# The conv branch's output product by seven block products instead of eight, its second-half gates read back half a tile at a time

## What is computed

```python
h = rmsnorm(x, norm_mix)
proj = h @ w_in + b_in                        # val, gate, pool_in, gate_a, gate_b
u = val * sigmoid(gate)
u = silu(layernorm(causal_dwconv31(u)))       # z below
ya = u @ conv_w_out                           # the product that is changed, 1024 x 1024 x 1024
yb = pool_branch(pool_in)                     # trailing means, one map per group
merged = sigmoid(gate_a) * ya + sigmoid(gate_b) * yb
x = x + merged @ mix_w_out                    # "the mix"
x = x + gdfn(rmsnorm(x))                      # up-projection, conv of 3, gelu * gate, down-projection
return rmsnorm(x)
```

## Time and profile before

| what | us |
|---|---|
| median of 3 runs (1289.60 to 1290.78) | 1289.91 |
| the profiled execution | 1289.33 |
| its span, first to last instruction | 1287.3 |
| PE busy | 1270.3 |
| DVE busy | 1022.8 |
| POOL busy | 871.1 |
| ACT busy | 479.5 |

### The profile page before, as it was taken

The page is one execution under the profiler, slowest core; times in us unless marked ns, Lnnn a source line. Parts: engine busy times, 40 slices in busy tenths (PEclk is TensorE's granted clock), DMA queues, the critical chain, the costliest instruction groups (busy, mean ns, idle before and its releaser), DMA issues.

```text
span 1287.3 us, 15571 instructions
## 1 busy us (share of the span) xinstructions
PE 1270.3 (99%) x5766; PEld 1053.8 (82%) x5766; DVE 1022.8 (79%) x1163; ACT 479.5 (37%) x691; POOL 871.1 (68%) x579
## 2 busy tenths in 40 slices
PE   8999999999999999999999999999999999999997
PEld 8888888888888778877888888888888888888887
DVE  5898989999999784589677767677666779887975
ACT  6211221213234580143445343343344445424551
POOL 4536637665787833478739977877887876567861
PEclk9999999999999999999999999999999999999999
DMA  9411121214334372344212322332232259868923
GB/s 352 149 33 49 34 82 49 82 33 164 99 99 149 130 290 69 114 155 164 102 39 90 123 107 92 121 121 88 93 117 107 90 175 361 332 243 290 367 87 131
DMA packets 66408, 179.26 MB, mean 139 GB/s; under 512 B 4896, under 2 KB 13088, under 8 KB 62496
## 3 DMA queue, kind: packets, MB, share of 16 engines
q1 hardware_dynamic: 61888, 167.82, 36.2%
q10 hardware_dynamic: 4448, 10.49, 2.2%
HBM read 137.14 MB, written 41.16 MB: 139 GB/s over the span
## 4 chain that ended last, share of the span: by engine, by line
PE 90%; DVE 4%; ACT 2%; issue 2%; POOL 1%; DMA 1%; SPq 0%; DVEq 0%; POOLq 0%; ACTq 0%
PE ps L2494 30%; PE ps L2495 30%; PE ps L2496 30%; DMA cv<-in_x 1%; DVE h_lo L2092 1%; POOL w_lo L1037 1%; PE ps L2558 1%; ACT cv L1244 0%; PE ps L2548 0%; DVE cv L2083 0%; ACT cv_r L1626 0%; DVE hi_f L2004 0%; POOL w_lo L1170 0%; DVE res L2271 0%; DVE res L2187 0%
## 5 line engine op out<-in xcount | busy, mean ns | idle before, releaser
L2494 PE MATMUL ps<-h_lo,w_hi 128*128 128x512 f32 (+1 forms) x900 | 348.0, 387 | 4.5 <-DVE h_lo L1838 1.9
L2496 PE MATMUL ps<-h_hi,w_hi 128*128 128x512 f32 (+1 forms) x900 | 345.9, 384 | 0.0
L2495 PE MATMUL ps<-h_hi,w_lo 128*128 128x512 f32 (+1 forms) x900 | 345.9, 384 | 0.0
L2494 PEld LDWEIGHTS ps<-h_lo,w_hi 128*128 128x128 f32 x900 | 169.0, 188 | 41.8 <-DVE h_lo L1838 3.1
L2496 PEld LDWEIGHTS ps<-h_hi,w_hi 128*128 128x128 f32 x900 | 169.0, 188 | 33.9
L2495 PEld LDWEIGHTS ps<-h_hi,w_lo 128*128 128x128 f32 x900 | 169.1, 188 | 33.1
L1918 DVE SCALAR_TENSOR_TENSOR ps<-tmp,par,ps 128x512 f32<-128x512 f32 x224 | 158.5, 750 | 0.0
L965 POOL TENSOR_SCALAR w_hi<-raw 128x1024 fp32r<-128x1024 f32 x32 | 36.5, 1141 | 156.1 <-issue 127.5
L2494 PE MATMUL ps<-ga_r,w_hi 128*128 128x512 f32 (+1 forms) x303 | 117.4, 388 | 0.3 <-POOL w_lo L1170 0.3
L2496 PE MATMUL ps<-cv_r,w_hi 128*128 128x512 f32 (+1 forms) x303 | 117.1, 386 | 0.0
L2495 PE MATMUL ps<-cv_r,w_lo 128*128 128x512 f32 (+1 forms) x303 | 117.0, 386 | 0.0
(11 more groups left out here) (308 smaller groups left out, 2721.3 us busy)
## 6 DMA issues: line engine op xcount, KB each, us to landing
raw<-in_wstream SPq DMA_DIRECT2D x54, 512.0 KB, 3.5
tmp<-in_wffn SPq DMA_DIRECT2D x14, 1024.0 KB, 4.7
g_kept<-res SPq DMA_DIRECT2D x21, 512.0 KB, 2.8
res<-in_wffn SPq DMA_DIRECT2D x10, 1024.0 KB, 4.8
ga_r<-g_kept SPq DMA_DIRECT2D x18, 512.0 KB, 7.0
h_lo<-g_kept SPq DMA_DIRECT2D x17, 512.0 KB, 7.5
res<-in_xT SPq DMA_DIRECT2D x7, 1024.0 KB, 5.8
g_kept<-raw SPq DMA_DIRECT2D x12, 512.0 KB, 2.9
```

Source lines behind the costliest of these rows:

```text
L2494: nc.tensor.matmul(out, a_hi, b_lo, start=start, stop=False, skip_group_check=onto)
L2495: nc.tensor.matmul(out, a_lo, b_hi, start=False, stop=False, skip_group_check=onto)
L2496: return nc.tensor.matmul(out, a_hi, b_hi, start=False, stop=stop, skip_group_check=onto)
```

## The change

The conv branch's output product is done by seven products over four pairs of output tiles too. P1 and P2 run for all four pairs; the other five for pairs 0 and 1 and then for 2 and 3. POOL makes its weight sums and lows (28 + 16 operations of 128x512), ACT its 28 highs, DVE its T sums, T lows and posts. Its T2 stays in PSUM (four banks), T1, T3 and T4 lie in `ga` and `cv`. The gates come back as 16 half tiles into four slots in `cv`, each asked for when the merge four places before has multiplied. The merged tiles are merged by halves, and their splits go to `h_hi` and `h_lo` half by half. The lists of calls are rewritten accordingly, those of the mix's start too; the weight block for the mix's pair 1 lies in `raw`.

```diff
+CONV_SEQ = [(p, i) for p in (P1, P2) for i in range(MP)]
+CONV_SEQ += [(p, a + i) for a in (0, 2) for p in (P6, P5, P7, P4, P3) for i in range(2)]
+MERGES = [(what, a + i) for a in (0, 2) for what in ("c11", "c22", "c21", "c12") for i in range(2)]
...
+        def conv_t2(k):
+            return bank((4, 5, 6, 1)[k])
+        def conv_bank(p, i):
+            if p in (P1, P2):
+                return bank((2, 3, 7, 0)[i])
+            return bank(((4, 5), (6, 1))[i % 2][p in (P5, P3)])
...
+            def gates_back(j):
+                what, i = MERGES[j]
+                m, h = 2 * i + int(what[1]) - 1, int(what[2]) - 1
+                if j == 0:
+                    sp.wait_ge(z_lo, KT + KT // 2)
+                    sp.wait_ge(t_sum, CONV_TS + 2 * KT)
+                if j >= 4:
+                    sp.wait_ge(co_a, j - 4 + 1)
...
+                sp.dma_start(a_slot[j % 4], a_dram[:, m, h * HALF:(h + 1) * HALF]).then_inc(pos_loaded[j % 4], 16)
...
+            for j in range(4):
+                gates_back(j)
+            for i in (2, 3):
+                sp.wait_ge(f_sum, conv_summed(i - 2, "S4"))
+                load_conv_quarter(i, 0, f_wlo, conv_op(P6, i - 2) + 1)
+            gates_back(4)
+            gates_back(5)
+            for i in (2, 3):
+                load_conv_quarter(i, 2, f_wlo, conv_op(P7, i - 2) + 1)
+            for i in (2, 3):
+                load_conv_quarter(i, 3, f_wlo, conv_op(P4, i - 2) + 1)
...
-            for s, i in enumerate((1, 3)):
-                sp.wait_ge(f_wlo, mix_op(P2, i) + 1)
+            sp.wait_ge(f_wlo, mix_op(P3, 1) + 1)
+            for s in range(2):
                 load_weights(N_FFN + s)
...
+            conv_low(P1, 0)
+            conv_sum("S1", 0)
+            conv_sum("S3", 0)
+            conv_low(P1, 1)
+            conv_sum("S2", 0)
+            conv_sum("S1", 1)
+            conv_sum("S3", 1)
+            conv_low(P1, 2)
+            conv_low(P1, 3)
+            conv_sum("S2", 1)
+            for i in range(MP):
+                conv_low(P2, i)
...
                 if what == "S1":
-                    pool.wait_ge(mx_c[i], 16)
-                    if i == 3:
-                        pool.wait_ge(f_used, mix_op(P1, 3) + 1)
+                    pool.wait_ge(mx_c[i], 48)
+                    if i == 0:
+                        pool.wait_ge(co_m, len(MERGES))
...
             z_high(0, 0, 1)
             ln_silu(7)
-            z_high(0, 2, 3, 4, 5, 6, 7)
-            z_high(1, 0, 1, 2, 3, 4, 5, 6, 7)
+            z_high(0, 2, 3)
+            conv_high(P1, 0)
+            conv_high(P1, 1)
+            z_high(0, 4, 5, 6, 7)
+            conv_high(P1, 2)
             gate_a1(5)
...
             ln_scaled(7)
+            for k in range(4):
+                conv_t_sum("T1", k)
             z_low(0, 0, 1, 2, 3)
+            for k in range(2):
+                conv_t_sum("T3", k)
             gate_c21(5)
+            for k in range(2, 4):
+                conv_t_sum("T3", k)
+            gate_c12(5)
+            for k in range(4):
+                conv_t_sum("T2", k)
             z_low(0, 4, 5, 6, 7)
-            gate_c12(5)
-            z_low(1, 0, 1, 2, 3, 4, 5, 6, 7)
             gate_pooled(5)
+            z_low(1, 4, 5)
+            for k in range(4):
+                conv_t_sum("T4", k)
+            z_low(1, 6, 7)
+            for k in range(4):
+                conv_t2_low(k)
+            conv_t_low("T1")
...
+            conv_u2_of(2)
+            merged_low(0, 0)
+            merged_low(1, 0)
+            conv_u2_of(3)
+            merge("c11", 2)
+            merge("c11", 3)
+            merged_low(2, 0)
+            merged_low(3, 0)
+            for k in range(4):
+                mix_t_sum_of("T1", k)
+            conv_c22(2)
+            merge("c22", 2)
+            merged_low(4, 0)
+            conv_c22(3)
...
+            conv_c12(3)
+            merge("c12", 3)
+            mix_t_sum_of("T3", 2)
+            for m in (5, 7, 4, 6):
+                merged_low(m, 1)
+            for k in (1, 3, 0, 2):
+                mix_t_sum_of("T2", k)
...
+            for k in (1, 3):
+                mix_t_sum_of("T4", k)
             mix_t_low("T3")
+            for k in (0, 2):
+                mix_t_sum_of("T4", k)
             mix_add("P2 0 11")
             mix_t_low("T2")
...
-            pairs(N_OUT, (((f_post, gate_posted(GP - 2, "c12")),),
-                          ((s1_out, gates_read(GP - 1, 1)), (f_post, gate_posted(GP - 1, "c21")))), co_m, h_hi, h_lo,
-                  lambda h, k: (z_lo, KT * h + k + 1))
+            for i in range(MP):
+                pe.wait_ge(*((f_post, gate_posted(GP - 2, "c21")), (f_post, gate_posted(GP - 2, "c12")),
+                             (s1_out, gates_read(GP - 2, 1)), (s1_out, gates_read(GP - 1, 1)))[i])
+                conv_product(P1, i, ready=(lambda k: (z_lo, k + 1)) if i == 0 else None)
+            for i in range(MP):
+                pe.wait_ge(f_v1, GP + i + 1)
+                conv_product(P2, i, False, ready=(lambda k: (z_lo, 4 + k + 1)) if i == 0 else None)
+            for a in (0, 2):
+                for i in (a, a + 1):
+                    if a:
+                        pe.wait_ge(co_m, merged("c21", i - 2))
+                    elif i == 0:
+                        pe.wait_ge(t_sum, CONV_TS + 2 * KT)
+                        pe.wait_ge(t_lo, CONV_THS + KT // 2)
+                    conv_product(P6, i)
...
```

More of the change, by code:

```diff
@@ L55 @@
 N_OUT = 5 * KT
-N_FFN = N_OUT + KT
+N_FFN = N_OUT
 N_UP = 2 * PLAIN
@@ new lines, in build, with conv_weights, z_part @@
+        a_slot = [cv[:, 6 * SEQ + i * HALF:6 * SEQ + (i + 1) * HALF] for i in range(4)]
+        def conv_weights(p, i):
+            if p == P1:
+                return block_quarter(i, 0) if i < 2 else csum[:, span(i - 2)[0]:span(i - 2)[1]]
+            if p == P2:
+                return block_quarter(i, 1) if i < 2 else second_half(lo_f, i)
+            return conv_s1[i % 2] if p == P5 else block_quarter(i, {P6: 0, P3: 1, P7: 2, P4: 3}[p])
+        def z_part(c, h):
+            return together(tile(cv, c))[:, h * PART:(h + 1) * PART, :]
@@ new lines, in _ @@
+            conv_first(1)
+            conv_high(P2, 1)
+            z_high(1, 6, 7)
+            conv_t2_high(0)
+            conv_t2_high(1)
+            conv_first(2)
+            conv_high(P2, 2)
+            conv_t2_high(2)
+            conv_t2_high(3)
+            conv_first(3)
+            conv_high(P2, 3)
+            conv_high(P6, 0)
+            conv_t_high("T1")
+            conv_high(P6, 1)
+            conv_t_high("T3")
+            conv_high(P5, 0)
+            conv_t_high("T4")
+            for p, i in CONV_SEQ[CONV_SEQ.index((P5, 1)):CONV_SEQ.index((P4, 1)) + 1]:
+                conv_high(p, i)
@@ new lines, in _ @@
+            conv_u2_of(0)
+            conv_t_low("T3")
+            conv_u2_of(1)
+            conv_t_low("T4")
+            merge("c11", 0)
+            merge("c11", 1)
+            for i in range(2):
+                conv_c22(i)
+                merge("c22", i)
+            for i in range(2):
+                conv_c21(i)
+                merge("c21", i)
+            for i in range(2):
+                conv_c12(i)
+                merge("c12", i)
+            conv_u2_of(2)
+            merged_low(0, 0)
@@ new lines, in _ @@
+            merged_low(1, 0)
[10 more added lines that the diff above has]
+            conv_c22(3)
+            merge("c22", 3)
+            conv_c21(2)
+            merge("c21", 2)
+            mix_t_sum_of("T3", 1)
+            merged_low(5, 0)
@@ L2959, in lay_out @@
         pairs.append(block)
-    pairs += [np.concatenate([mix[2 * i], mix[2 * i + 1]], axis=1) for i in range(MP)]
+    pairs += [np.concatenate([w[2 * i], w[2 * i + 1]], axis=1) for w in (out, mix) for i in range(MP)]
+    for half in (slice(0, HALF), slice(HALF, CH)):
+        pairs.append(np.concatenate([mix[2 * i][:, half] for i in range(MP)], axis=1))
     ffn_stream = np.ascontiguousarray(np.concatenate(pairs, axis=0))
```

606 lines of the change are left out of this document (412 added, 194 removed).

## The result

The changed kernel takes 1305.8 us (median of 4 runs, 1305.5 to 1307.2), the kernel before beside it 1289.8; the ratio is 1.0124, 95% interval 1.0111 to 1.0136. So it is 16.0 us slower; the forecast was 11.1 above the median of before. The profiled execution took 1305.5, its span is 1303.7, 16.4 more than the span of before.

A forecast was written before the change was run, and what follows sets the result against it. TensorE was taken to bound the kernel. Saved matmuls (10.88 us) were outweighed by waits at the conv start (12.0), middle (3.7) and mix (10): +11.3 on 1289.33 gave 1300.6, as median 1301; range 1286 to 1306.

The forecast's parts named there:

- Start, steps 1 and 2: Conv stage's start: POOL's first split at 467.3, P1 0 at 469.0; eight POOL operations make P1 2 4.7 to 8.3 late.
- a sign that I had put under "wrong": Signs against the forecast: T sums of 0.7 beside busy POOL, T2's into PSUM at 0.7, POOL's first split before 467.
- signs for "right": Conv start: PE idle 8 to 10 us before P1 1, P1 2, P2 0; DVE's T sums and z lows at 1.7.
- Start, step 3: Conv start: DVE's queue alternates with POOL, z_low(0,7) ends at 490.3, P2 0 waits at its fourth step; P2 3 10.2 late.
- Start, step 4: Conv start: P6 0 waits for T sums and four T2 lows until 501.1, 12.0 late; 8.5 if PSUM-writing T2 is free.
- Middle: Rest of the conv stage: waits at P7 0 1.0, P6 2 0.7, P4 2 0.9, P4 3 1.1; sum 3.7, from 0 to 7.
- Last merge: Between conv stage and mix: c12(3) merged about 5 us behind the stage's end, at 564.
- The chain: DVE behind the last merge: 27 us beside POOL, to 591, a stall of 10; without POOL it would end in time.
- Behind the T2 product: After the mix's first T2 product: same order as before, 1 off for POOL's full ring, 0.3 added for up-projection weights.
- absorbed: Rival: operations of DVE and POOL meet less than the queues suggest, start costs only 4.8; 1283.5 us, chance 0.20.
- The mix in time: Rival: earlier last merge or POOL idling between mix sums leaves 4 to 6 of 10; chance 0.22, shared with T2 free.
- Late loads: Rival: quarters for S1 1 or behind gates 4 and 5 land late, S1 and P6 2 wait 5 to 8 more; chance 0.08.

The follow-up runs named there:

- start_mid: Changed kernel with start_order's order at the conv stage's start, mended, and POOL's splits P3 1 and P6 2 moved ahead of sums mid-stage; 1305.9 us.
- mix_psum: Changed kernel with the DVE operations behind the last merge reading their second operand from PSUM instead of SBUF (values not right); 1292.0 us.
- both_psum: Changed kernel with the edits of t_psum and mix_psum together, no order changed (values not right); 1289.8 us, ratio to the kernel before 1.0003.
- mix_hold: mix_order with POOL also held behind the split of P4 0 until DVE's T2 low in the mix; 1303.3 us.
- mix_order: Changed kernel with POOL's mix sums for pair 0 made between the splits of P1, and P2 0's copy and split before the last merges; 1304.0 us.
- keep_busy: Changed kernel with useless matmuls of 512 columns put into the places where PE waits; 1309.7 us.
- t_psum: Changed kernel with the conv branch's T1, T3 and T2 sums reading one operand from PSUM instead of SBUF (values not right); 1301.6 us.
- start_order: Changed kernel with the same operations in another order on POOL, DVE and ACT at the conv stage's start; 1305.8 us.
- all_orders: Changed kernel with the edits of start_mid and mix_hold together, no operation added or removed; 1302.8 us.

## Why the forecast came out as it did

The direction and the main mechanism were right, and the sum was 4.8 too small. The measured time is just inside the upper bound of 1306. In the profile the span grew by 16.4 where the sum has 11.3, 5.1 more: start -0.6, middle +2.3, last merge +2.9, chain -0.9, PE's start behind the chain +0.1, behind the T2 product +1.2. Terms that were 6.5 too small stand against 1.5 that was too large. Step by step:

- **What is removed**: 48 matmuls, as counted.
- **Start, steps 1 and 2.** Forecast: POOL's first split at 467.3, P1 0 at 469.0, P1 2 late by 4.7 to 8.3. Measured: the split starts earlier, at 466.69, but lasts 3.66, so P1 0 starts at 470.45, and P1 2 at 482.46, 9.7 late. I had let an operation of POOL take 1.7 at most when DVE is full. So a sign that I had put under "wrong" (a first split before 467) did come, and no gain with it. The signs for "right" came in part: PE idles 2.8 before P1 0 and 3.4 before P1 2, not before P1 1 or P2 0, together 6.2 and not 8 to 10.
- **Start, step 3.** Wrong place: z_low(0,7) was to end at 490.3 and to stop P2 0 at its fourth step. It ended at 486.3, and P2 0 did not wait. P1 2 and P1 3 had been late enough. start_mid shows the limit of step 4 by itself: with P1 and P2 on time, P6 0 would still come at 495.3.
- **Start, step 4.** Right to 0.6 us (501.1 forecast, 500.48 measured), partly by luck, since it was POOL's order that set it, not DVE's chain: P6 0 follows P2 3 without a wait, 1.2 after the last T2 low (499.24). In DVE's chain two errors met: it reached the end of z_low(0,7) 4.0 early, and from there to the last T2 low it took 13.0 where I had 10.8. The value I chose for T2's sums in PSUM was right: they took up to 1.8 and 1.66 in the mean, and 0.70 once one input was in PSUM too. The Trainium skill (SBUF — State Buffer, "SBUF: two separate sides") puts the lock on the two SBUF inputs, and the trace agrees.
- **Middle.** Forecast 3.7, measured 6.0 (560.92 - 500.48 - 20 x 2.72): P6 2 2.2 in place of 0.7, since POOL's sums wait for quarters that are loaded behind the gates (POOL idle for 4.4 to 518.00) and eight of its operations stand between that and P6 2's split; P6 3 another 1.4 that I had not seen, slow matmuls behind that wait, and 0.3 within P6 3; P4 2 0.4 for 0.9; P4 3 1.6 for 1.1; P7 0 nothing for 1.0.
- **Last merge.** 7.7 us behind the stage's end, not 5. DVE takes up P3 2's result at 561.57, 3.4 after that product has ended; this is the term that was mis-sized most. I had counted what follows the last product, not the work of DVE still queued in front of it.
- **The chain.** 27 forecast, 26.1 measured; the sentence that it would end in time without POOL is shown by mix_psum (T2 low at 579.4, PE there at 581.5).
- **Behind the T2 product.** Forecast -0.7, measured +0.5: the slow matmuls behind the long wait (2.2) are what I had left out, and without them it would be -1.7. No wait shows at the up-projection's weights, which I had given 0.3.

The rivals: "absorbed" is out in this kernel, and both_psum shows what it would have needed. "The mix in time" did not come; its condition, a POOL that idles between its mix sums, did not hold: from 568.79 to 590.83 POOL's operations follow each other without a wait, and it idles (3.7) only behind them. "Late loads" did come in a mild form, 1.5 us at P6 2, not the 5 to 8 that it wanted. The gates' loads, costed at nothing, cost nothing: none of PE's waits is released by a merge.

**Left open.** How the 1 us behind the mix in mix_hold comes about; whether the chain could be moved to PSUM operands with right values, for which all eight banks would have to be planned anew. I did not try either.

## What to carry to other kernels

Before matmuls are traded for sums and splits, list the added DVE operations by how many SBUF inputs they have, and price each one with two (of 128x512) at the 1.7 us that it took here beside a busy POOL, not at 0.6; then ask for each of them whether an operand could lie in PSUM. A reordering helps only where the next limit lies well behind: here 6 us gained at the conv stage's first product on T2 were all lost 36 us later. And when another engine has work ready for the whole stretch, moving its operations out brings others in; it has to be held back, and then its own work comes late.

## What the chip showed that I had not expected

- **A waiting POOL operation can be passed over.** In the changed kernel POOL's first split, by its length and where it ends, waits through four DVE operations with two SBUF inputs that follow each other without a gap (a z low just begun, one more, two T3 sums), and gets through when DVE comes to an operation with a PSUM input (L2278). The same order gave 3.64 in mix_order, 3.65 in mix_psum and 3.72 in keep_busy. In t_psum, where the T3 sums behind the z lows have a PSUM input, the split took 2.38, and in start_order, where L2278 stands at its place, 1.83. Only after the first turn do the two alternate.

```profile
465.44 2.56 DVE L2375 TENSOR_TENSOR h_lo<-cv,h_hi 128x512 fp32r<-128x512 f32 x4
466.69 3.66 POOL L1253 TENSOR_TENSOR w_lo<-tmp,w_hi 128x512 fp32r<-128x512 f32 x1 [4.00 <-ACT w_hi L1661]
467.90 1.31 DVE L2394 TENSOR_TENSOR ga<-cv 128x512 f32<-128x512 f32 x2
469.12 0.70 DVE L2278 TENSOR_TENSOR tmp<-ps,lo_f 128x512 f32<-128x512 f32 x1
```

- **PE's clock falls after waits of a few microseconds.** Behind the waits of 2.8, 3.4, 2.0, 2.1 and 6.4 us matmuls start 0.427 us apart instead of 0.227 for some microseconds. The granted clock there is 0.50 (at 471 to 475, 484 to 486, 585.8 to 588 and 595 to 599), which is the 1.2 GHz level in place of 2.4. It falls sometimes at once (594.88), sometimes up to 1.5 us after PE has resumed. Behind the mix's wait of 2.1 us:

```profile
584.31 0.47 PE L2898 MATMUL ps<-h_lo,w_hi 128*128 128x512 f32 x1 [2.07 <-POOL w_lo L1316]
584.62 0.39 PE L2899 MATMUL ps<-h_hi,w_lo 128*128 128x512 f32 x1
...
585.77 0.62 PE L2898 MATMUL ps<-h_lo,w_hi 128*128 128x512 f32 x1
586.19 0.63 PE L2899 MATMUL ps<-h_hi,w_lo 128*128 128x512 f32 x1
```

The length of the wait alone does not decide it: behind waits of 1.88 (t_psum) and 1.85 (both_psum) before P6 2 a slow stretch followed (clock 0.50 and 0.51 at 527 to 530), behind one of 1.67 at the same place in mix_psum, one of 1.90 in mix_order and one of 2.26 in all_orders none did (1.00 at 565 to 572 in the last two). Where the clock falls, a stall costs its own length and up to 2.2 us more; where another wait follows soon, that is hidden in it.
